# Attention B of a hybrid encoder block: its value products in two column halves, its row sums by a product with ones

## The chip, the cores and the metric

One core of a Trainium2 chip runs the whole program. The time is device microseconds from start to end of one execution; the medians are over three executions.

## The reference

One residual block on 1024 positions of width 1024, all in float32. A combined projection gives the inputs of two attention branches and two gates; the branches are projected, gated, added, projected again and added to x; then an MLP of width 4096. The change lies in branch B, eight heads of causal latent attention:

```python
s = jnp.einsum('bqhd,bkhd->bhqk', qi, k).astype(jnp.float32) * scale
s = jnp.where(key_chunk[None, :] <= q_chunk[:, None], s, -jnp.inf)
p = jax.nn.softmax(s, axis=-1).astype(v.dtype)
return jnp.einsum('bhqk,bkhd->bqhd', p, v)
```

Queries and keys have 96 numbers a head, values 64. Key chunks of 64 are causal as wholes.

## The kernel before, in words

All engines run lists of instructions written out by hand, which meet at semaphores. The stages follow one another: the input projection, the gates with attention A interleaved, attention B, the branch projections, the output projection, the MLP.

**Slots.** Attention B holds scores transposed, keys on partitions and queries along the free axis. A head has `HEAD_SLOTS` = 12 slots of one tile of 128 keys: slots 0 to 3 are the first half of the queries (512 of them) against key tiles 0 to 3, slots 4 to 7 the second half against key tiles 0 to 3 (full squares), slots 8 to 11 the second half against key tiles 4 to 7. The first and the last four are on the diagonal and have 512, 384, 256 and 128 columns. Eight heads make 96 slots. A slot number within a head is called r below.

**TensorE**, slot by slot (loop from L1698 on): `scores_t` makes the scores in three products of split numbers (L1638 to L1640) into one of two banks; `values_t` of the slot two before (L1643 to L1659) multiplies the exponentials with the values; `approx` (L1622) makes one chunk of the next head's approximate scores, whose row maxima DVE takes (`row_max`, L2090 to L2099) and SP moves into the row of queries; then come the steps of `preparations`: the projections of a later pair of heads (`group_step`, p 0 to 7) in the odd heads 1 and 3 and its transposes (p 8 to 15) in the even heads 2 and 4, for the second pair of heads both in head 0. Step p 7 falls into r 10 of an odd head (r 3 of head 0), p 12 into r 6 of the even head after it (r 9 of head 0).

**The value product** has 65 stationary columns, 64 of values and one of ones, so that row 64 of its result is the softmax's sum:

```python
out = PS[0:V_DIM + 1, 5 + u % 2, :]
ins = pe.matmul(out[:, c0:HALF], vB[g % 3][:, kt, h % B_GROUP, :], p_tile(t)[:, c0:HALF],
                start=kt == 0, stop=last)
```

**ScalarE** takes the exponentials (`exp_b`, L1321 to L1324), copies a half head's result out of its bank (`y_out`), and rounds it for the split (`y_high`, L1344). **SP** moves the sums from a row to a column (L718), stores the reciprocals (L723) and spreads them over 64 partitions (L728). **DVE** takes the reciprocals (L2105), multiplies (`y_norm`, L2115) and makes the low parts (`y_low`, L2122); each comes at a fixed slot of its own list. **GpSimd (POOL)** normalises the prepared queries and keys in a chain for each half of a group (`b_power`, `b_scale`, `b_rotate`, L879 to L984), which TensorE's transposes p 8 and p 12 wait for (`b_normed`); behind its second chain it splits attention A's output (L1012, L1014), and after the last chain it splits the branch weights (L870, L872).

**Behind the stage** come 16 branch products (`branch`, 24 products each, L1452). The fifth, e 4, waits for branch B's output (`yB_ready`), for its weights (`bw_ready`), and for the first gate multiplication (`gate_mul`), which DVE does after its last `y_low`. SP issues at the stage's end: three fetches of stored gates, the last sums, their reciprocals and the spread, a fourth gate, four loads of branch weights.

Of the kernel before, what the change touches and what calls it, by code (L numbers as in the profile page):

```python
# [62 lines left out]
P_RING = 3  # L63
# [24 lines left out]
def build(nc, x, positions, g_mix, w_in, b_gate, g_qa, g_ka, sinks_a, g_cq, g_ckv,  # L88
# [6 lines left out]
    with ExitStack() as ctx:  # L95
# [41 lines left out]
        b_sum = const("b_sum", [P, 2, Q_BLOCK])  # L137
# [6 lines left out]
        for t_ in (ident, b_gate_c, g_qa_c, g_ka_c, gqk_a, g_cq_c, g_ckv_c, g_qb_c, g_kb_c,  # L144
                   gqk_b, g_qr, g_kr, sink_r, pos_i, pos_c, inv_f, minus_half, x_ss, x_ms, x_rstd, z_ss, z_ms,
                   z_rstd, b_ss, b_ms, b_rstd, cos_t, sin_t, kr_rot, a_nmax, a_sum, a_rsum, b_nmax, b_part, b_sum,
                   b_rsum, probe):
# [50 lines left out]
        rtmp = [place(f"rtmp{i}", 199.875 + 0.5 * i, [P, 4, B_GROUP, RH]) for i in range(4)]  # L198
        vB = [place(f"vB{i}", (195.75, 202, 66.25)[i], [P, T, B_GROUP, V_DIM + 1]) for i in range(3)]
# [8 lines left out]
        p_diag = [place(f"p_diag{i}", 40 + 2 * i, [P, HALF]) for i in range(Q_BLOCK)]  # L208
        p_full = [place(f"p_full{i}", 48 + 2 * i, [P, HALF]) for i in range(P_RING)]
        r_row = [place(f"r_row{i}", 54 + 2 * i, [P, HALF]) for i in range(2)]  # L210
        y_raw = [place(f"y_raw{i}", 58 + 2 * i, [P, HALF]) for i in range(2)]

        yT_hi = [place(f"yT_hi{j}", (72, 76, 80, 84, 88, 128, 136, 140.75)[j], [P, S], F32R) for j in range(8)]
        yT_lo = [place(f"yT_lo{j}", (161, 165, 169, 173, 92, 132, 202, 144.75)[j], [P, S], F32R) for j in range(8)]
        b_raw = [place(f"b_raw{i}", 153 + 2 * i, [P, 4, P]) for i in range(BW_RING)]
# [32 lines left out]
        r_d = nc.dram_tensor("r_store", (2, P, Q_BLOCK), F32, kind="Internal").ap()  # L248
# [66 lines left out]
        v_one_ready = sem("v_one_ready")  # L315
# [7 lines left out]
        slot_done = sem("slot_done")  # L323
        y_raw_ready = sem("y_raw_ready")
        sum_landed = [sem(f"sum_landed{i}") for i in range(2)]
# [145 lines left out]
        def block_end(u):  # L471

            return HEAD_SLOTS * (u // 2) + (Q_BLOCK if u % 2 == 0 else HEAD_SLOTS)

        def diagonal(t):

            h, half, kt, c0 = slot(t)
            return kt >= Q_BLOCK * half

        def p_tile(t):  # L480

            h, half, kt, c0 = slot(t)
            return p_diag[kt - Q_BLOCK * half] if diagonal(t) else p_full[(Q_BLOCK * h + kt) % P_RING]

        def p_tile_before(t):

            h, half, kt, c0 = slot(t)
            if diagonal(t):
                return t - T if half else t - Q_BLOCK
            n = Q_BLOCK * h + kt - P_RING  # L490
            return HEAD_SLOTS * (n // Q_BLOCK) + Q_BLOCK + n % Q_BLOCK
# [15 lines left out]
        def chunk_at(t):  # L507

            h, r = t // HEAD_SLOTS, t % HEAD_SLOTS
            return N_CHUNKS * (h + 1) + r if h + 1 < B_HEADS else None  # L510

# [106 lines left out]
        def _(sp):  # L618
# [92 lines left out]
            def sum_row(u):  # L711

                r = 0 if (u // 2) % 2 else V_DIM
                return y_raw[u % 2][r:r + 1, :]

            def sum_move(u):
                sp.wait_ge(y_raw_ready, u + 1)
                sp.dma_start(b_sum[:, u % 2, :], sum_row(u).rearrange("o (p t) -> o p t", t=Q_BLOCK)  # L718
                             ).then_inc(sum_landed[u % 2], 16)

            def reciprocal_store(u):
                sp.wait_ge(rsum_b_ready, u + 1)
                sp.dma_start(r_d[u % 2], b_rsum[:, u % 2, :]).then_inc(r_stored, 16)  # L723

            def reciprocal_spread(u):
                s, r = u % 2, V_DIM * ((u // 2) % 2)
                sp.wait_ge(r_stored, 16 * (u + 1))
                sp.dma_start(r_row[s][r:r + V_DIM, :],  # L728
                             r_d[s].rearrange("p t -> (p t)").rearrange("(o q) -> o q", o=1).partition_broadcast(V_DIM)
                             ).then_inc(r_landed[s], 16)  # L730
# [19 lines left out]
            for h in range(B_HEADS):  # L750
# [4 lines left out]
                if h == 1:  # L755
                    for e in range(BW_RING):
                        branch_load(e)
                if more:
                    nmax_move(h + 1, 0, 1, 2)
                if h:  # L760
                    sum_move(2 * h - 1)
                if more:
                    nmax_move(h + 1, 3)
                if h:
                    reciprocal_store(2 * h - 1)
                if more:
                    nmax_move(h + 1, 4)
                if h:
                    reciprocal_spread(2 * h - 1)
                sum_move(2 * h)  # L770
                if more:
                    nmax_move(h + 1, 5)
                reciprocal_store(2 * h)
                if more:
                    nmax_move(h + 1, 6)
                reciprocal_spread(2 * h)
# [82 lines left out]
        def _(pool):  # L859
            pool.memset(ident[:, :], 0.0).then_inc(ident_ready, 1)  # L860
            pool.memset(minus_half[:, :], -0.5).then_inc(const_ready, 1)
            for i in range(RH):
                pool.memset(inv_f[:, i:i + 1], INV_FREQ[i]).then_inc(const_ready, 1)
# [152 lines left out]
            for n in range(2, 2 * B_GROUPS):  # L1016
# [3 lines left out]
                if n == 3:  # L1020
# [3 lines left out]
                    for j in range(4):  # L1024
                        yA_lanes(j)
# [10 lines left out]
            for e in range(2 * KD):  # L1036
                branch_splits(e)
# [1302 lines left out]
```

## Time and profile before

| | us |
|---|---|
| median of 3 runs | 1387.34 (1387.0 to 1388.23) |
| profiled execution, its own time | 1388.76 |
| its span, first to last instruction | 1386.9 |
| TensorE busy | 1364.9 (98%) |
| VectorE (DVE) busy | 814.6 (59%) |
| GpSimd (POOL) busy | 761.0 (55%) |
| ScalarE (ACT) busy | 407.8 (29%) |
| granted TensorE clock | 0.998 of full |

The profiled execution took 1.42 us more than the median. Busy times are unions over the whole span; attention B runs from 373 us to 545 us of it. A full float32 product leaves two records in the trace, a product of rounded float32 numbers one, so "x2" at a value product is one product. Starts of records are measured; the ends of matmul records are modelled and overlap the next record, so the chain's pieces are the better price of one product.

### The profile page before, as it was taken

How to read it: one execution, taken by the hardware profiler on the slowest of the kernel's cores; microseconds unless marked ns; L12 is line 12 of the kernel's file. 1: busy time of each engine (PE TensorE's matmuls, PEld its weight loads, DVE VectorE, ACT ScalarE, POOL GpSimd, SP SyncE). 2: the span in 40 equal slices, each digit the busy share in tenths (PEclk: the TensorE clock that was granted, in tenths of full speed). 3: DMA queues.
4: the chain of work that ended last, by engine and by line, in shares of the span. 5: the costliest groups of instructions: out<-in, count | busy, mean ns of one | idle time of the engine just before them, and what ended most of it. 6: DMA issues, size and time to landing. Idle time of an engine off the chain costs nothing.

```text
span 1386.9 us, 17629 instructions
## 1 busy us (share of the span) xinstructions
PE 1364.9 (98%) x6660; PEld 1119.9 (81%) x6660; DVE 814.6 (59%) x1422; ACT 407.8 (29%) x857; POOL 761.0 (55%) x618
## 2 busy tenths in 40 slices
PE   8999999999999999999999999999999999999998
PEld 8999887668867766888887888888888888888887
DVE  5401725743577773455356667777667776666776
ACT  5113235642355654000133212221221222221121
POOL 2341924445384520454308666668766667866697
PEclk9999999999999999999999999999999999999999
DMA  7120231211120012735101112111111221111113
GB/s 240 39 62 16 88 95 61 65 61 46 41 46 16 9 17 62 247 107 199 29 28 49 53 40 60 61 53 40 53 54 45 61 62 39 53 54 53 47 46 122
DMA packets 102884, 90.82 MB, mean 65 GB/s; under 512 B 21904, under 2 KB 84880, under 8 KB 102800
## 3 DMA queue, kind: packets, MB, share of 16 engines
q1 hardware_dynamic: 102656, 89.17, 21.0%
q8 instruction: 53, 0.87, 0.3%
q10 hardware_dynamic: 144, 0.52, 0.1%
q14 instruction: 31, 0.25, 0.1%
HBM read 76.99 MB, written 12.62 MB: 65 GB/s over the span
## 4 chain that ended last, share of the span: by engine, by line
PE 89%; POOL 3%; DVE 3%; ACT 2%; issue 1%; DMA 1%; ACTq 0%; DVEq 0%; POOLq 0%
PE PS L1452 76%; PE PS L1658 3%; PE PS L1459 2%; PE PS L1833 1%; PE PS L1553 1%; PE PS L1555 1%; PE PS L1638 1%; PE PS L1639 1%; PE PS L1622 1%; PE PS L1640 1%; POOL gw_lo L928 1%; DVE scA L2059 1%; POOL b_rstd L879 1%; PE PS L1575 1%; PE PS L1590 0%
## 5 line engine op out<-in xcount | busy, mean ns | idle before, releaser
L2243 DVE TENSOR_TENSOR xr<-PS,xr 128x512 f32<-128x512 f32 x240 | 161.9, 685 | 80.5 <-PE PS L1452 80.5
L2243 DVE TENSOR_TENSOR sum<-PS,sum 128x512 f32<-128x512 f32 x168 | 114.3, 687 | 91.3 <-PE PS L1452 91.3
L1452 PE MATMUL PS<-w_hi,u_hi 128*128 128x512 f32 x420 | 163.6, 390 | 0.8 <-DVE u_lo L2247 0.8
L1452 PE MATMUL PS<-w_lo,u_hi 128*128 128x512 f32 x420 | 163.4, 389 | 0.0
L1452 PE MATMUL PS<-w_hi,u_lo 128*128 128x512 f32 x420 | 163.4, 389 | 0.0
L1058 POOL TENSOR_TENSOR w_lo<-w_raw,w_hi 128x512 fp32r<-128x512 f32 x109 | 156.2, 1433 | 9.1
L1452 PE MATMUL PS<-mT_hi,w_hi 128*128 128x512 f32 x512 | 160.4, 389 | 0.0
L1452 PE MATMUL PS<-mT_hi,w_lo 128*128 128x512 f32 x512 | 160.2, 389 | 0.0
L1452 PE MATMUL PS<-mT_lo,w_hi 128*128 128x512 f32 x512 | 160.2, 389 | 0.0
L1387 ACT ACTIVATE relu_t<-PS 128x512 f32<-128x512 f32 x64 | 38.3, 599 | 296.7 <-PE PS L1452 293.8
L870 POOL TENSOR_SCALAR w_hi<-w_raw 128x1024 fp32r<-128x1024 f32 x32 | 39.4, 1230 | 155.7 <-DMA w_raw<-in_w_ff 155.7
L1452 PEld LDWEIGHTS PS<-mT_hi,w_lo 128*128 128x128 f32 x512 | 96.1, 188 | 20.0
L1452 PEld LDWEIGHTS PS<-mT_hi,w_hi 128*128 128x128 f32 x512 | 96.1, 188 | 19.9
L1452 PEld LDWEIGHTS PS<-mT_lo,w_hi 128*128 128x128 f32 x512 | 96.1, 188 | 19.9
L1452 PEld LDWEIGHTS PS<-w_hi,u_hi 128*128 128x128 f32 x420 | 78.8, 188 | 17.9 <-DVE u_lo L2247 1.6
L1395 ACT ACTIVATE u_hi<-u_raw 128x512 fp32r<-128x512 f32 x60 | 36.3, 629 | 191.4 <-DVE u_raw L2254 137.6
L1452 PEld LDWEIGHTS PS<-w_hi,u_lo 128*128 128x128 f32 x420 | 78.9, 188 | 16.4
L1452 PEld LDWEIGHTS PS<-w_lo,u_hi 128*128 128x128 f32 x420 | 78.9, 188 | 16.3
L1061 POOL TENSOR_TENSOR w_raw<-w_raw 128x512 f32<-128x512 f32 x60 | 80.1, 1336 | 18.2 <-PE PS L1452 15.2
L1452 PE MATMUL PS<-hT_hi,gw_hi 128*128 128x512 f32 x256 | 84.4, 411 | 3.5 <-ACT gate L1213 2.3
L1054 POOL TENSOR_SCALAR w_hi<-w_raw 128x512 fp32r<-128x512 f32 x109 | 87.7, 805 | 0.0
L2247 DVE TENSOR_TENSOR u_lo<-u_raw,u_hi 128x512 fp32r<-128x512 f32 x77 | 82.0, 1065 | 0.8 <-ACT u_hi L1390 0.8
(237 smaller groups left out, 2966.9 us busy)
## 6 DMA issues: line engine op xcount, KB each, us to landing
w_raw<-in_w_ff SPq DMA_DIRECT2D x32, 512.0 KB, 4.0
w_raw<-in_w_ff SPq DMA_DIRECT2D x64, 256.0 KB, 2.6
g_raw<-in_w_in SPq DMA_DIRECT2D x16, 512.0 KB, 3.9
gate_store<-gate SPq DMA_DIRECT2D x16, 512.0 KB, 2.6
x_in<-in_x SPq DMA_DIRECT2D x8, 512.0 KB, 10.7
gate_a<-gate_store SPq DMA_DIRECT2D x8, 512.0 KB, 7.6
gate_b<-gate_store SPq DMA_DIRECT2D x8, 512.0 KB, 4.8
raw<-in_w_out SPq DMA_DIRECT2D x8, 512.0 KB, 3.6
```

Of the source, the lines that this page charges most:

```text
L870: pool.tensor_scalar(hi_ap, raw_ap, 1.0, 1.0, ALU.mult, ALU.mult).then_inc(hi_done, 1)
L879: return pool.tensor_tensor(out_ap, in_ap, e, ALU.pow)
L1054: pool.tensor_scalar(w2_hi[b][:, :], w2_raw[b][:, :], 1.0, 1.0, ALU.mult, ALU.mult).then_inc(w2_step, 1)
L1058: pool.tensor_tensor(w2_lo[b][:, :], w2_raw[b][:, :], w2_hi[b][:, :], ALU.subtract).then_inc(w2_step, 1)
L1061: pool.tensor_tensor(w2_raw[AT[out]][:, :], w2_raw[AT[a]][:, :], w2_raw[AT[b]][:, :], ALU.subtract).then_inc(w2_step, 1)
L1387: act.activation(relu_t[:, :], PS[:, 2 * tile + half, :], ACT.Relu).then_inc(u_act, 1)
L1395: act.activation(u_hi[AT[p]][:, :], u_raw[AT[p]][:, :], ACT.Copy).then_inc(u_act, 1)
L1452: ins = pe.matmul(o, st, cut(mv), start=first and n == 0, stop=last and n == 2)
L1459: ins = pe.transpose(PS[0:rows, bank, i * P:(i + 1) * P], ap, ident[:, :])
L1658: ins = pe.matmul(out[:, c0:HALF], vB[g % 3][:, kt, h % B_GROUP, :], p_tile(t)[:, c0:HALF], start=kt == 0, stop=last)
L2243: dve.tensor_tensor(out, part, out, ALU.add).then_inc(acc_done, 1)
L2247: dve.tensor_tensor(u_lo[AT[p]][:, :], raw_ap, u_hi[AT[p]][:, :], ALU.subtract).then_inc(u_vec, 1)
```

## The change

The value tiles have 64 columns, without the ones. The twelve exponential tiles of a head have twelve places of their own (`p_set`, three sets of four) instead of four and a ring of three. The value products come in groups of four, one group every fourth slot at r 2, 6 and 10, for the four slots before; within a group they go by turns to PSUM partitions 0 to 63 and 64 to 127 of one bank. The two half results are added: ACT copies one out (`y_out`), DVE adds the other from PSUM (`y_add`).

For the sums, POOL adds the four tiles of the first set (`sums_first`, one multiplication and three additions) and those of the last set (`sums_last`, three additions), DVE adds the full tiles in pairs (`full_add`, two additions of 128x512). Four products with a 128x32 tile of ones, each into 32 partitions of the second half's bank, make the four sums (`sums`), at r 7 of the next head; for the last head behind branch product e 0. ACT copies that bank out, SP moves four rows, DVE adds three of them and takes two reciprocals. Multiplication, rounding and low parts come at slots 34 to 37 counted from the head's start. On POOL the additions stand between the chains; attention A's splits move to heads 5 and 6, the first four branch weight splits to heads 6 and 7, the loads of these weights to head 5 on SP.

```diff
             def y_out(u):
-                act.wait_ge(slot_done, block_end(u))
-                if u >= 2:
-                    act.wait_ge(yB_ready, u - 1)
+                act.wait_ge(group_done, 3 * h + 1 + 2 * half)
...
+            def sums_out(h):
+                act.wait_ge(s_done, h + 1)
+                if h:
+                    act.wait_ge(sum_landed, 64 * h)
+                act.activation(s_raw[:, :], PS[:, sums_bank(h), :], ACT.Copy).then_inc(s_read, 1)
...
+            def values_group(j):
+                h, part = j // 3, j % 3
+                half = min(part, 1)
+                u, g = 2 * h + half, h // B_GROUP
+                pe.wait_ge(p_ready, Q_BLOCK * (j + 1))
+                if part < 2 and u >= 2:
+                    pe.wait_ge(y_added, u - 1)
+                if part == 1 and h:
+                    pe.wait_ge(s_read, h)
...
+                for i in range(Q_BLOCK):
+                    own = (i % 2, i in (1, 2))[part != 1]
+                    c0 = P * i if part != 1 else 0
+                    rows = head_rows(h) if own else other_rows(h)
+                    ins = pe.matmul(PS[rows, 5 + half, c0:HALF], vB[g % 3][:, i + Q_BLOCK * (part == 2), h % B_GROUP, :],
+                                    p_set[part][i][:, c0:HALF], start=part < 2 and i < 2, stop=part != 1 and i >= 2)
+                ins.then_inc(group_done, 1)
+
+            def sums(h):
+                bank = sums_bank(h)
+                pe.wait_ge(sum_step, SUM_STEPS * (h + 1))
+                pe.wait_ge(full_added, 2 * (h + 1))
+                if h < B_HEADS - 1:
+                    pe.wait_ge(y_added, 2 * h + 2)
...
+                for i, p in enumerate((first_sum(h), p_sum[1], p_sum[2], p_set[2][0])):
+                    ins = pe.matmul(PS[32 * i:32 * i + 32, bank, :], ones_w[:, :], p[:, :], start=True, stop=True)
+                ins.then_inc(s_done, 1)
...
             for t in range(N_SLOTS):
                 scores_t(t)
-                if t >= 2:
-                    values_t(t - 2)
+                if t > Q_BLOCK and t % Q_BLOCK == 2:
+                    values_group(t // Q_BLOCK - 1)
                 a = chunk_at(t)
                 if a is not None:
                     approx(a)
+                if t > HEAD_SLOTS and t % HEAD_SLOTS == SUM_AT:
+                    sums(t // HEAD_SLOTS - 1)
                 for g, p in preparations(t):
                     group_step(g, p)
-            values_t(N_SLOTS - 2)
-            values_t(N_SLOTS - 1)
+            values_group(3 * B_HEADS - 1)
...
             for e in range(2 * KD):
                 branch(e)
+                if e == 0:
+                    sums(B_HEADS - 1)
...
+            chain(2)
+            chain(3)
+            sums_first(0)
+            for h in range(1, B_HEADS):
+                sums_last(h - 1)
+                sums_first(h)
+                if h in (1, 3):
+                    chain(h + 3)
+                    chain(h + 4)
...
+            def y_steps(t):
+                for h in range(B_HEADS):
+                    r = t - HEAD_SLOTS * h
+                    if r == 9:
+                        y_add(2 * h)
+                    if r == 17:
+                        y_add(2 * h + 1)
+                    if r in (10, 11):
+                        full_add(h, r - 10)
+                    if r == 24:
+                        sum_reciprocal(h)
+                    if r in (34, 35):
+                        y_norm(2 * h + r - 34)
+                    if r in (36, 37):
+                        y_low(2 * h + r - 36)
...
             for d in range(3):
                 fetch_a(d)
-            sum_move(BLOCKS - 1)
-            reciprocal_store(BLOCKS - 1)
-            reciprocal_spread(BLOCKS - 1)
+            reciprocal_store(B_HEADS - 2)
+            reciprocal_spread(B_HEADS - 2)
+            sum_move(B_HEADS - 1)
+            reciprocal_store(B_HEADS - 1)
+            reciprocal_spread(B_HEADS - 1)
             fetch_a(3)
```

## Rows read from the trace of the kernel before

**Rows 1.** The page: busy time by engine, and the chain by engine.
```profile
PE 1364.9 (98%) x6660; PEld 1119.9 (81%) x6660; DVE 814.6 (59%) x1422; ACT 407.8 (29%) x857; POOL 761.0 (55%) x618
...
PE 89%; POOL 3%; DVE 3%; ACT 2%; issue 1%; DMA 1%; ACTq 0%; DVEq 0%; POOLq 0%
```

**Rows 2.** Six heads: stretch, length, then PE, PEld, DVE, ACT, POOL busy us.
```profile
373.00:399.70 26.70, 24.60 (x126) 17.94 (x125) 20.10 (x61) 15.37 (x39) 22.94 (x26) 1.00 0.13 33
399.70:425.00 25.30, 25.30 (x123) 19.38 (x121) 17.93 (x63) 14.31 (x40) 18.64 (x16) 1.00 0.29 67
425.00:446.40 21.40, 20.68 (x106) 14.07 (x105) 17.49 (x44) 13.40 (x34) 10.20 (x11) 1.00 0.09 14
...
492.90:510.90 18.00, 17.13 (x74) 10.99 (x73) 12.56 (x31) 9.51 (x28) 7.56 (x7) 1.00 0.09 15
510.90:528.40 17.50, 16.84 (x74) 10.96 (x73) 11.04 (x30) 8.87 (x24) 0.00 (x0) 1.00 0.11 17
528.40:544.80 16.40, 15.61 (x66) 9.46 (x65) 4.65 (x10) 9.08 (x27) 0.00 (x0) 1.00 0.12 17
```
**Rows 3.** The chain of waits, heads 1 and 2: start, us, what.
```profile
424.29 0.55 ACT sqB L1265
...
426.36 2.92 POOL b_rstd L879
...
436.94 0.61 PE PS L1459 x4
437.79 0.24 PE PS L1639
438.26 0.86 PE PS L1658 x2
```

**Rows 4.** The chain in attention A, at its 64-column value products.
```profile
242.66 0.58 PE PS L1606 x4
```

**Rows 5.** Groups of instructions by shape: busy us, mean ns, idle before.
```profile
L1324 ACT ACTIVATE p_full<-PS 128x512 f32<-128x512 f32 x32 | 18.9, 596 | 4.9 <-PE PS L1640 4.5
...
L2122 DVE TENSOR_TENSOR yT_lo<-y_raw,yT_hi 64x512 fp32r<-64x512 f32 x14 | 9.8, 699 | 1.6 <-ACT yT_hi L1344 1.5
...
L2115 DVE TENSOR_TENSOR y_raw<-y_raw,r_row 64x512 f32<-64x512 f32 x14 | 11.7, 838 | 9.5 <-DMA r_row<-r_store 9.4
...
L972 POOL TENSOR_TENSOR q_nat<-q_nat,g_qr 128x256 f32<-128x256 f32 x4 | 2.9, 728 | 0.0
...
L2247 DVE TENSOR_TENSOR u_lo<-u_raw,u_hi 128x512 fp32r<-128x512 f32 x77 | 82.0, 1065 | 0.8 <-ACT u_hi L1390 0.8
```

**Rows 6.** POOL in order of time: the chain for step p 12 of head 0.
```profile
385.61 2.91 POOL L879 TENSOR_TENSOR b_rstd<-b_ms,minus_half 128x16 f32<-128x16 f32 x1 [0.40 <-DVE b_ms L2047]
...
394.64 0.45 POOL L984 TENSOR_TENSOR q_nat<-rtmp 128x128 f32<-128x128 f32 x1
```

**Rows 7.** Busy us by engine, r 7 to 11 of head 2.
```profile
437.30:446.40 9.10, 9.10 (x46) 6.00 (x45) 6.85 (x18) 5.42 (x13) 0.00 (x0) 1.00 0.08 17
```

**Rows 8.** SP's queue in order of time behind the stage.
```profile
546.30 0.75 SPq L718 DMA_DIRECT2D b_sum<-y_raw  x1
554.01 0.32 SPq L723 DMA_DIRECT2D r_store<-b_rsum  x1
555.42 0.47 SPq L728 DMA_DIRECT2D r_row<-r_store  x1
...
556.56 0.43 SPq L737 DMA_DIRECT2D b_raw<-in_w_branch_b  x1
```

**Rows 9.** DVE, then POOL, in order of time behind the stage.
```profile
561.53 0.69 DVE L2122 TENSOR_TENSOR yT_lo<-y_raw,yT_hi 64x512 fp32r<-64x512 f32 x1 [0.69 <-ACT yT_hi L1344]
...
562.68 0.62 POOL L870 TENSOR_SCALAR bw_hi<-b_raw 128x512 fp32r<-128x512 f32 x1 [61.97 <-DMA b_raw<-in_w_branch_b]
563.39 1.30 POOL L872 TENSOR_TENSOR bw_lo<-b_raw,bw_hi 128x512 fp32r<-128x512 f32 x1
```

**Rows 10.** The chain behind the stage: the branch products.
```profile
544.80 55.35 PE PS L1452 x244
```

More of the change, by code:

```diff
@@ L322, in build @@
         p_ready = sem("p_ready")
-        slot_done = sem("slot_done")
-        y_raw_ready = sem("y_raw_ready")
-        sum_landed = [sem(f"sum_landed{i}") for i in range(2)]
+        group_done = sem("group_done")
+        sum_step = sem("sum_step")
+        full_added = sem("full_added")
+        s_done = sem("s_done")
+        s_read = sem("s_read")
+        y_copied = sem("y_copied")
+        y_added = sem("y_added")
+        sum_landed = sem("sum_landed")
         rsum_b_ready = sem("rsum_b_ready")
@@ L1014, in yA_lanes, with chain @@
                 pool.tensor_tensor(yT_lo[j][:, :], yTa[:, j, :], yT_hi[j][:, :], ALU.subtract).then_inc(yA_split, 1)
-            for n in range(2, 2 * B_GROUPS):
+            def chain(n):
                 b_power(n)
@@ L1035, in branch_splits @@
                 split(b_raw[s][:, :, :], bw_hi[s][:, :, :], bw_lo[s][:, :, :], bw_hi_done, e + 1, bw_ready)
-            for e in range(2 * KD):
+            chain(2)
[7 more added lines that the diff above has]
+                    chain(h + 4)
+                if h == 5:
+                    pool.wait_ge(gate_done, 2 * KD)
+                    pool.wait_ge(pv_done, N_A // 2)
+                    pool.wait_ge(y_ready, N_A)
+                    for j in range(3):
+                        yA_lanes(j)
+                if h == 6:
+                    yA_lanes(3)
+                    branch_splits(0)
+                    branch_splits(1)
+                if h == 7:
+                    branch_splits(2)
+                    branch_splits(3)
+            sums_last(B_HEADS - 1)
+            for e in range(4, 2 * KD):
                 branch_splits(e)
@@ new lines, in y_add, with y_steps @@
+            def y_add(u):
+                h, half = u // 2, u % 2
+                c = 0 if half else P
+                y = y_raw[h // 2][head_rows(h), y_cols(half, c)]
+                dve.wait_ge(y_copied, u + 1)
+                dve.tensor_tensor(y, PS[head_rows(h), 5 + half, c:HALF], y, ALU.add).then_inc(y_added, 1)
+            def y_steps(t):
+                for h in range(B_HEADS):
+                    r = t - HEAD_SLOTS * h
+                    if r == 9:
[10 more added lines that the diff above has]
+                        y_low(2 * h + r - 36)
@@ L2147, in _ @@
             dve.wait_ge(gate_done, 2 * KD)
-            for i in range(Q_BLOCK):
-                dve.memset(p_diag[i][CHUNK:P, i * P:i * P + CHUNK], 0.0).then_inc(p_zero_ready, 1)
+            for part in (0, 2):
+                for i in range(Q_BLOCK):
+                    dve.memset(p_set[part][i][CHUNK:P, i * P:i * P + CHUNK], 0.0).then_inc(p_zero_ready, 1)
             for t in range(N_SLOTS):
```

273 lines of the change are left out of this document (141 added, 132 removed).

## The prediction

> **What bounds the kernel now.** The page first: TensorE is busy in 98% of the span and is 89% of the chain [rows 1], so only TensorE's own time, or a new wait of it, counts. The change touches 373 to 545 us, so next the busy time head by head [rows 2]. Head 1 has TensorE busy in all of its 25.30 us, DVE in 17.93. Head 2 has TensorE idle for 0.7 of 21.40 and DVE busy for 17.49; heads 5 and 6 have DVE at 12.56 of 18.00 and 11.04 of 17.50. Head 7, without approximations and preparations, has DVE at 4.65 of 16.40. The chain [rows 3] shows a second bound. From the projection copies of step p 7 (ACT, 424.29) through POOL's chain (from 426.36) to TensorE's transposes of p 12 (436.94) runs a latency of 12.65 us, and TensorE waits at its end. Head 0 has the same at r 9: POOL's second chain starts 0.4 us behind its first and ends at 395.09, whatever TensorE does before [rows 6].
>
> **Values.** One full value product takes 0.86 us of the chain [rows 3], so 0.43, 0.64 and 0.21 us for 256, 384 and 128 columns by proportion. A head has 4,608 columns in all: 9 x 0.86 = 7.74 us. Two 64-column products of 256 columns, side by side in attention A, took 0.58 us together [rows 4], where one after the other would be 2 x 0.43 = 0.86. So the halves do run at once, for 0.43 + 0.15 us of switching. I take 0.15 at either end of a group, 0.3 us. A group of four full tiles puts 1,024 columns on a side: 1.72 + 0.3 = 2.0 us; a diagonal one 640: 1.07 + 0.3 = 1.37. A head: 4.75 us, 3.0 less than now.
>
> **Sums.** Four products of 512 columns in four quarters: no row has 32-column tiles. All at once is 0.86 + 0.3 = 1.15 us; one after the other 3.4 + 0.3 = 3.7. I take 1.15, since rows 4 are the nearest and show no loss between two. TensorE's net per head is 1.9 us less.
>
> **DVE.** New per head: two 128x512 additions from SBUF, two from PSUM of 512 and 384 columns, a reduction. A 64x512 low part takes 0.70 us; 128x512 low parts in the MLP, beside a busy POOL, 1.07 [rows 5]. So a full addition is 0.70 to 1.07, the PSUM ones 0.69 and 0.55, the reduction with its link some 0.25: 2.9 to 3.6 us, I take 2.9. Its cover is DVE's idle time, large in heads 1 and 7, small in 2 and 5.
>
> **POOL.** 256 columns take 0.73 us [rows 5], so additions of 384, 256 and 128 about 1.0, 0.73 and 0.46 us: 2.2 us for a last set, 2.6 for a first one with its multiplication. They fit into heads 1, 3, 5, 6, 7, where POOL has over 6 us free [rows 2]. In the even heads the last set stands behind the chain.
>
> **ACT and SP.** ACT has one sum copy more and one-row copies less, 9 to 15 us busy of 16 to 27 [rows 2]; nothing. SP's 15 issues per head against 14, beside 16 us or more, cost nothing while the maxima go before the sums, as they do in its list.
>
> **Head by head.**
> Head 0: the wait at r 9 ends at 395.1 as before. Before, eight value products were done in its shadow; now the group of r 6 alone is, and that of r 10 comes behind it: 2.0 us against the 1.5 that slots 10 and 11 have now. **+0.5.**
> Heads 1 and 3, to step p 7 in r 10: now 7.1 us of value products; then the groups of r 2, 6, 10 and a sum, 1.37 + 1.37 + 2.0 + 1.15 = 5.9. -1.1; lean slots are as long for DVE as for TensorE, so I take **-0.8 each**.
> From p 7 to p 12 the 12.65 us stand: 0; TensorE only waits longer.
> Heads 2 and 4, r 7 to 11: 9.1 us, DVE 6.85 [rows 7]. TensorE has 4.1 us of values now, then 2.0 + 1.15, -0.9. DVE gets 0.69 + 1.4 more and loses 0.36: 8.6 of 9.1, so little of it comes through. The last set starts when the chain ends and takes 2.2 us plus its links, while TensorE gets to the sums about 1.3 us after the transposes: a wait of 1.0. **+0.9 each.**
> Head 5: DVE goes to 15.5, TensorE's 18.0 to 16.1; both are near. **-0.7.** Head 6: DVE 14 of 15.6: **-1.1.**
> Head 7: TensorE alone has scores 36 x 0.24 = 8.6 at most (narrow ones less: 6.8), values 4.75, sums 1.15, but lean slots are held by the exponential: three score products of 0.24, an exponential of 0.60 [rows 3, 5] and two hand-overs make 1.7 us per two slots, some 1.2 us of waits. The last group waits for the last exponential, 0.5. 14.4 for 16.40: **-2.0.**
>
> **Behind the stage.** The last head's sums stand among the branch products: **+1.15.** And what follows them is later. A branch product e takes 24 x 55.35/244 = 5.45 us [rows 10], so e 4 comes 21.8 us behind the end of the values, 23.0 with the sums. Now the spread is issued at +10.8 (555.42), the weights of e 4 land at +18.1 and are split at +20.1 [rows 8, 9]. New: sums done at +6.6, copied at +7.4, four moves issued by +9.7 and landed 2 us later, reciprocals at +12.3, stored, spread issued at +13.7 and +14.2, weights landed some 7 us behind: +21.4, split at +23.4. On DVE two norms and two low parts stand behind the spread's landing: last low part near +21, first gate multiplication 1.2 later. Today's sums were late because they queued behind the gate fetches (7.5 us from 546.30 to the reciprocal); the new ones come when these are through. A wait of 0 to 3 us; I take **+0.8.**
>
> **Sum:** 0.5 - 1.6 + 0 + 1.8 - 0.7 - 1.1 - 2.0 + 1.15 + 0.8 = -1.15 us, against 1388.76 of the profiled execution; against the median 1387.34 it makes 1386.2.
>
> **A rule against the change.** L2115 takes 0.84 us on average in the stage, where the same shape in L2122 takes 0.70 [rows 5]: some of its operations were held up. The Trainium skill, "SBUF — State Buffer", section "Who interferes with whom", says that a DVE operation with two SBUF inputs and a GpSimd one that reads SBUF exclude each other, the later one waiting in full. The new full additions and POOL's additions are of these kinds; it is the mechanism beside the second rival.
>
> **The rivals.**
> *TensorE's gain comes through where I let DVE take it* (chance 0.36). For it: rows 2 show DVE with slack in every whole head. Then -1.1 twice, -0.9 and no wait at the sums twice, -1.9 twice, -2.0, +0.5, +1.15, nothing behind: -8.1, 1379. Against it: DVE reads in order, and TensorE may be only two approximations ahead.
> *DVE becomes the bound* (0.23), the slower one. Place: r 7 to 11 of even heads and all of heads 5 and 6, where DVE and POOL now both work on SBUF. Price: full additions at 1.07, the eight y operations 0.15 longer each: 4.3 us per head. It decides when DVE's 8.6 of 9.1 us exceeds the stretch; 4.3 in place of 2.9 does. Then nothing is won in heads 1, 3, 5, 6, even heads lose 2.0 each, head 7 keeps -2.0, the tail waits 3: 0.5 + 4.0 - 2.0 + 1.15 + 3 = +6.7, 1394.
> *The quarters do not run at once* (0.04): 2.6 us more eight times, +20 less what hides: 1400 or more. Rows 4 speak against it.
> That the halves are not at once I leave out: rows 4 exclude it.
>
> **Numbers.** My case, within a few us of none, 0.37. About 0.2%, 2.8 us, is what a measurement of this kernel can tell from no change. Faster 0.36, same 0.37, slower 0.27. The range 1378 to 1394 holds both first rivals and leaves out the serial quarters and a full 15 us (8 x 1.9).
>
> **What would show it.** Value groups of 1.4 and 2.0 us and sums of 1.15 us in TensorE's order of time; longer waits for POOL's chain at r 9 of head 0 and r 6 of heads 2 and 4; TensorE waiting for POOL's additions at r 7 of these; DVE above 85% in heads 2 to 6; head 7 near 14.4 us; e 4 starting 23 us or more behind the last values. A DVE with idle time in heads 5 and 6 and a stage shorter by over 5 us would be the first rival; idle TensorE before approximations and transposes, with full additions of 1 us, the second.

## The result and the profile after

The changed kernel took 1400.99 us (median of 4 runs, 1399.63 to 1401.86) against 1387.76 us for the kernel before on the same chip: a ratio of 1.0092, with 95% interval 1.008 to 1.0104. It is slower, and the time lies outside the range. The profiled execution took 1401.86 us.

The page of after, busy time, granted clock and chain, which answers to [rows 1]:

```profile
PE 1363.9 (97%) x6724; PEld 1115.1 (80%) x6724; DVE 835.0 (60%) x1463; ACT 408.9 (29%) x857; POOL 799.3 (57%) x675
...
PEclk9999999999999998999999999999999999999999
...
PE 88%; DVE 5%; POOL 3%; ACT 2%; issue 1%; DMA 0%; DVEq 0%; POOLq 0%; ACTq 0%
```

Two things differ. DVE's share of the chain is 5% instead of 3%. And one slice of the clock row has an 8: TensorE did not have its full clock there. One slice is 35 us long, so this row hides short stretches. The windows by head of after (the columns are those of [rows 2], the last three being granted clock, DMA share and GB/s) show them:

```profile
371.84:402.39 30.55, 24.39 (x122) 17.30 (x121) 20.73 (x65) 15.68 (x39) 20.89 (x26) 0.89 0.11 29
402.39:426.15 23.76, 23.76 (x131) 18.24 (x129) 17.86 (x60) 13.36 (x38) 13.86 (x18) 1.00 0.09 16
426.15:447.63 21.48, 18.89 (x113) 12.95 (x112) 16.76 (x44) 12.49 (x32) 14.20 (x18) 1.00 0.09 14
447.63:472.93 25.30, 24.36 (x129) 18.11 (x128) 20.32 (x66) 14.11 (x42) 14.22 (x18) 1.00 0.09 12
472.93:496.72 23.79, 20.63 (x114) 13.93 (x112) 20.25 (x48) 13.97 (x34) 15.32 (x18) 0.93 0.09 13
496.72:514.99 18.27, 15.79 (x82) 9.84 (x80) 13.54 (x36) 8.98 (x27) 12.62 (x12) 1.00 0.31 74
514.99:539.51 24.52, 21.33 (x82) 13.62 (x81) 16.71 (x36) 9.01 (x26) 15.19 (x15) 0.72 0.08 11
539.51:556.22 16.71, 15.03 (x77) 8.48 (x75) 9.77 (x20) 10.07 (x29) 8.72 (x11) 1.00 0.13 24
```

The windows of the two heads of the kernel before that [rows 2] left out, 3 and 4:

```profile
446.40:471.60 25.20, 25.20 (x122) 19.26 (x121) 18.18 (x62) 14.37 (x42) 9.26 (x11) 1.00 0.08 12
471.60:492.90 21.30, 20.60 (x105) 14.04 (x104) 17.38 (x44) 13.28 (x34) 10.91 (x13) 1.00 0.09 14
```

From first score product to first branch product the stage takes 184.4 us; before it took 171.5 (373.0 to 544.5). Heads 0, 4 and 6 have a granted clock of 0.89, 0.93 and 0.72, and head 6 alone is 7.0 us longer. Windows over the stretches themselves:

```profile
392.90:399.80 6.90, 5.75 (x16) 2.55 (x17) 1.21 (x2) 1.07 (x3) 3.33 (x7) 0.51 0.01 0
478.30:481.70 3.40, 3.40 (x14) 2.16 (x12) 3.23 (x11) 2.01 (x6) 3.32 (x4) 0.50 0.03 3
519.20:532.90 13.70, 13.21 (x39) 8.95 (x40) 9.25 (x23) 4.21 (x11) 9.02 (x11) 0.50 0.12 20
```

They are at 0.5, the lower level of 1.2 GHz: 24.0 us in all, in which TensorE is busy for 22.4. At 2.4 GHz that work would have taken half as long, so by estimate they cost **about 11.2 us**. The kernel before has no such stretch in the stage (1.00 in each window). Without them the stage would take some 173.2 us, still 1.7 more than before. Two checks that half is the right price here: head 6 took 24.5 us with 13.7 us at half clock, and 18.4 with none in the run of the filled waits below; head 0 took 30.5 with 6.9 at half clock, and 27.8 with none.

The PE column gives the whole account. Its rows add up to 165.7 us busy of 171.5 before (up to the first branch product) and to 164.2 of 184.4 after. Take the clock's 11.2 us off, and TensorE's own work fell by 12.7 us; its idle time rose by 14.4, from 5.8 to 20.2. So the idle time alone is more than the gain, and the clock's 11.2 us come on top: 12.9 us in all.

What comes ahead of each stretch is idle time of TensorE. Its waits in after, in order of time:

```profile
394.05 1.06 PE L1525 MATMUL PS<-ident,q_nat 128*96 128x128 f32 x4 [2.65 <-POOL q_nat L995]
...
519.69 0.58 PE L1688 MATMUL PS<-kT_hi,qT_hi 96*128 96x256 f32 x1 [3.19 <-DVE b_part L2182]
```

The first is the wait at r 9 of head 0. The second stands at r 1 of head 6, and head 4 has its like at r 1 (2.4 us). Heads 2 and 5 wait there too, for 1.6 and 1.5 us, and no half clock follows. A sum of TensorE's waits over the stage shows what is new:

```profile
PE PS L1688 <- DVE b_part L2182: 9.2, 5, 3.2
PE PS L1525 <- POOL q_nat L995: 3.6, 3, 2.7
PE PS L1688 <- DVE b_nmax L2179: 3.3, 5, 1.1
```

The approximation (L1688) waits 12.5 us for DVE's row maxima; before it waited 1.1 us for them in the whole stage. What DVE does at that time is seen in its order of time before the wait in head 6:

```profile
514.62 0.69 DVE L2182 TENSOR_REDUCE b_part<-PS 128x1 f32<-128x512 f32 x1 [1.23 <-PE PS L1688]
515.34 0.69 DVE L2232 TENSOR_TENSOR y_raw<-y_raw,r_row 64x512 f32<-64x512 f32 x1
516.06 2.73 DVE L2192 TENSOR_TENSOR p_sum<-p_set,p_set 128x512 f32<-128x512 f32 x1
518.80 0.11 DVE L2176 MEMSET PS<- 64x64 f32 x1
518.94 0.69 DVE L2182 TENSOR_REDUCE b_part<-PS 128x1 f32<-128x512 f32 x1
519.67 0.15 DVE L2185 TENSOR_REDUCE b_nmax<-b_part 128x1 f32<-128x2 f32 x1
```

Behind the row maximum of r 10 stand the division (L2232) and a full addition (L2192). Only then comes the maximum of r 11 that the approximation of r 1 needs. This full addition takes 2.73 us, the other in this stretch 0.69. POOL is in its low part then:

```profile
515.42 2.82 POOL L1025 TENSOR_TENSOR yT_lo<-yTa,yT_hi 128x1024 fp32r<-128x1024 f32 x1
```

DVE's operation began 0.6 us behind it and ended 0.6 us behind its end. By the rule of the Trainium skill, "SBUF — State Buffer", section "Who interferes with whom", that the prediction cited, the later of two such operations is held until the first ends; this trace agrees (2.73 against 0.69 us).

**TensorE's own instructions cost what was forecast.** A diagonal group, the four ones products and a full group, in order of time:

```profile
430.73 1.30 PE L1727 MATMUL PS<-p_set,vB 128*64 128x512 f32 x8
...
440.44 0.63 PE L1743 MATMUL PS<-p_sum,ones_w 128*32 128x512 f32 x3 [0.78 <-POOL p_set L1035]
440.46 0.62 PE L1743 MATMUL PS<-p_set,ones_w 128*32 128x512 f32 x1
440.89 0.60 PE L1743 MATMUL PS<-p_sum,ones_w 128*32 128x512 f32 x3
...
469.07 1.94 PE L1727 MATMUL PS<-p_set,vB 128*64 128x512 f32 x8
```

1.30 and 1.94 us against 1.37 and 2.0; the two passes of the ones products start 0.45 us apart, some 1.0 us in all against 1.15. Head 1, where TensorE is busy throughout in both kernels, shows the net: 1.5 us less, against the 1.9 of the prediction.

### The profile page after: what moved, and what is told of

The parts are those of the page before. It is cut to its first block, busy times and chain, and to the rows that moved or that the text cites. A ratio compares the mean times of both kernels' runs of the same rounds, so it can differ in the third digit from the quotient of the medians.

```text
span 1400.0 us, 17848 instructions
## 1 busy us (share of the span) xinstructions
PE 1363.9 (97%) x6724; PEld 1115.1 (80%) x6724; DVE 835.0 (60%) x1463; ACT 408.9 (29%) x857; POOL 799.3 (57%) x675
## 4 chain that ended last, share of the span: by engine, by line
PE 88%; DVE 5%; POOL 3%; ACT 2%; issue 1%; DMA 0%; DVEq 0%; POOLq 0%; ACTq 0%
PE PS L1518 75%; PE PS L1727 2%; PE PS L1525 2%; PE PS L1921 1%; PE PS L1619 1%; PE PS L1688 1%; PE PS L1704 1%; PE PS L1705 1%; PE PS L1621 1%; PE PS L1706 1%; POOL gw_lo L939 1%; DVE scA L2145 1%; PE PS L1641 1%; PE PS L1743 1%; DVE p_sum L2192 1%
## 5 line engine op out<-in xcount | busy, mean ns | idle before, releaser
L1518 PEld LDWEIGHTS PS<-w_hi,u_hi 128*128 128x128 f32 x420 | 78.8, 188 | 18.1 <-DVE u_lo L2355 1.8
```

Source lines behind the costliest of these rows:

```text
L1518: ins = pe.matmul(o, st, cut(mv), start=first and n == 0, stop=last and n == 2)
```

## The experiments

The letters in the later texts on record: A and B are two theories of the waits at r 1, C and D two of the clock. Ratios are against the kernel before, with 95% interval. "Stage" is the length as above (before 171.5, after 184.4), "half" the time at half clock in it (0 and 24.0), both of the one profiled execution; where the stretches fall differs between executions, so medians carry the verdicts. The runs were made on several chips, on which the kernel before took 1386.4 to 1387.9 us: medians of different groups of runs compare to about 1.5 us only, and the ratios are the fairer measure.

| run | median us | ratio | stage, half |
|---|---|---|---|
| filled waits | 1400.31 | 1.0092 (1.0075 to 1.0109) | 182.6, 17.1 |
| additions at r 14, 15 | 1407.62 | 1.0134 (1.0117 to 1.0151) | 195.5, 37.5 |
| low parts in pieces | 1397.29 | 1.0076 (1.006 to 1.0093) | 179.0, 17.1 |
| late additions, pieces, fills in head 0 | 1409.52 | 1.0153 (1.0136 to 1.017) | 192.0, 27.3 |
| no full additions | 1399.51 | 1.0103 (1.0074 to 1.0132) | 178.0, 13.7 |
| full additions on POOL | 1400.96 | 1.0113 (1.0091 to 1.0134) | 181.6, 23.9 |
| splits two slots later | 1395.69 | 1.0065 (1.0046 to 1.0085) | 179.4, 27.3 |
| four edits at once | 1392.34 | 1.0045 (1.0028 to 1.0062) | 174.4, 10.2 |
| groups last in slot | 1397.97 | 1.0067 (1.005 to 1.0083) | 180.9, 27.3 |
| division four slots later | 1392.55 | 1.0038 (1.0024 to 1.0052) | 173.3, 10.2 |
| all edits together | 1391.57 | 1.0032 (1.0022 to 1.0043) | 173.1, 6.8 |
| before, DVE held, 16 | 1392.31 | 1.0039 (1.0026 to 1.0051) | 175.0, 3.4 |
| before, DVE held, 24 | 1396.07 | 1.0065 (1.0048 to 1.0082) | 180.2, 10.2 |
| division later, filled | 1393.75 | 1.0044 (1.0027 to 1.0061) | 177.5, 13.7 |
| division later, ones at r 8 | 1396.24 | 1.0064 (1.0048 to 1.0081) | 178.9, 3.4 |
| the same, ones at r 7 | 1391.01 | 1.0036 (1.0022 to 1.0051) | 173.3, 10.2 |
| division later, lanes moved | 1392.86 | 1.0046 (1.002 to 1.0071) | 178.3, 13.7 |
| additions where room is | 1389.17 | 1.0018 (1.0009 to 1.0027) | 170.8, 6.8 |

**Filled waits.** TensorE multiplies the identity with itself into a free bank ahead of three waits.

```diff
+                    if (g, p) == (1, 12):
+                        keep_busy(bank, 12)     # and 11, 14 of them at slots 49 and 73
```

> The changed kernel with 12, 11 and 14 small products of the identity on TensorE in front of the three long waits (head 0 r 9, head 4 r 1, head 6 r 1), about as long as the waits. Clock theory (the half clock behind the three idle stretches, 24 us long, costs about 10 of the 13 us): the granted clock stays at full from 373 to 560 us and the time falls to about 1391 us. Order theory (the waits themselves cost it): the waits are still there, filled, so 1401 us within 2.

No gain: the time is the one of the order theory. That does not show this theory, since the half clock did not go. Head 0 was free of half clock (27.8 us, 2.7 fewer), but stretches of 3.4 to 6.8 us stood in heads 2, 4 and 5. Filling single waits moved the stretches.

**Full additions at r 14 and 15.**

```diff
-                    if r in (10, 11):
+                    if r in (14, 15):
```

> The two full additions of a head move from r 10 and 11, where DVE also has the two y_norm, to r 2 and 3 of the next head. Order theory: TensorE's wait for DVE at r 1 (1.6, 0.5, 2.4, 1.5, 3.2 us in heads 2 to 6) shrinks by about 1.4 us each, 5 to 7 us in all. Clock theory: these too, and the half clock of heads 4 and 6 goes with them: 8.5 us more of it, 1388 to 1390 us; the half clock of head 0 stays. If DVE is bound by its amount of work and not by the order, the waits move to r 3 and 4 and the time stays at 1400.

Worse by 6.6 us. The exponential that overwrites these tiles in the next head now waits for the additions, and TensorE for it: the sum of waits of this kernel begins with

```profile
PE PS L1704 <- ACT p_set L1379: 7.1, 6, 1.6
```

**POOL's low parts in four pieces of 256 columns.**

```diff
-                pool.tensor_tensor(yT_lo[j][:, :], yTa[:, j, :], yT_hi[j][:, :], ALU.subtract)
+                for c in range(0, S, 256):
+                    ins = pool.tensor_tensor(yT_lo[j][:, c:c + 256], ...)
```

> The four GpSimd subtractions of 128x1024 in heads 5 and 6 become sixteen of 128x256. If the 2.73 us of DVE's full addition in head 6 is the hold of the GpSimd operation of 2.8 us beside it, that addition falls to at most 1.4 us and TensorE's wait of 3.2 us to about 2. Clock theory: head 6's half clock goes too, 7 us; in all 1392 to 1394 us. Order theory: 1399 to 1400 us.

Its DVE row in place of the one of 2.73 us:

```profile
515.78 1.10 DVE L2194 TENSOR_TENSOR p_sum<-p_set,p_set 128x512 f32<-128x512 f32 x1
```

The division in front of it took 1.36 us in place of 0.69, so the two together fell from 3.4 to 2.5 us, and TensorE's wait behind them from 3.2 to 2.3. A piece takes about 1.0 us, and the trace shows no operation held for longer than that. The median fell by 3.7 us, between the two forecasts; the intervals of the two ratios overlap, so the size is not certain. The late additions, the pieces and the fills of head 0 at once:

> The additions later, the short subtractions, and the 12 small products in head 0 alone, together. Clock theory: full clock throughout, stage shorter than before by a few us: 1383 to 1388 us. Order theory: 1392 to 1395 us. DVE bound by amount: 1396 us or more.

The late additions decide that one.

**No full additions.** They are cut to 8 columns, so the sums of the full tiles are left out of the output.

> The changed kernel with DVE's full additions cut to 8 of 512 columns (so the sums of the full tiles are left out of the softmax's division; everything else runs). It takes some 11 us of DVE work out of 8 heads, at the slots where TensorE waits for DVE. DVE theory (the full additions at r 10 and 11 make row_max late, TensorE waits at r 1, and behind the idle stretches the clock halves): the waits at r 1 of heads 2 to 6 fall from 1.7, 0.6, 2.6, 1.7, 3.3 us to under 1 each, the half clock of heads 4 and 6 goes, 1386 to 1391 us. Rival (the order of TensorE's groups itself leaves it short of work in these heads, DVE or not): the waits and the half clock stay for the most part, 1397 us or more.

Little: the ratio is no better than the change's, and the waits at r 1 of heads 2, 4 and 6 are still 1.05, 1.89 and 2.65 us (1.6, 2.4 and 3.2 before the cut). The additions are not the root. Beside them stood these two:

> The full additions go from DVE to POOL, behind sums_first, in heads 1 and 3 between the two chains, where POOL had 4.5 us free; two additions of 128x512, 2.7 us a head. DVE theory: like the run without them, 1387 to 1392 us. If POOL becomes the bound (its additions late at r 7 of heads 2 and 4), 1395 us and waits for POOL at the sums. A complete computation.

> ACT's y_high and DVE's y_low two slots later each (r 1 to 3 of the next head but two in place of r 11 to 1), the full additions stay. ACT's exponentials at r 0 and 1 then do not stand behind a y_high that waits for DVE's y_norm. If that coupling makes the wait at r 1, it falls by 1 us and more in heads 3 to 6 and the time to about 1394 us; if DVE's amount of work before row_max makes it, little changes, 1398 to 1401 us.

On POOL, the additions gain nothing. With the splits (`y_high`, `y_low`) moved by two slots the median is 5.3 us lower, of which 1.4 are the faster chip; the waits at r 1 of heads 3 to 5 stayed, and only that of head 6 fell, from 3.2 to 1.1 us. These two with the pieces and 12 fills in head 0:

> Full additions on POOL, y_high and y_low two slots later, the GpSimd subtractions of 1024 columns in quarters, and 12 small products before the wait of head 0. DVE theory with the clock's price: no half clock or one short one, 1382 to 1387 us, at or under the kernel before. If TensorE's order is the rest, 1390 us or more.

It took 1392.34 us, the second of its forecasts. POOL's additions are now late: TensorE waits 2.1 us for them at the ones products that stand in head 6.

**Groups last in their slot**, behind approximation and projection.

> The change, with TensorE's group of value products issued at the end of its slot, behind the maximum's product and the projection or transposes, instead of ahead of them. Theory A (with the full additions cut to nothing the waits of slot 1 stood at 1.2 to 2.8 us, so the additions are not their root: the group at r 10, 1.8 us, stands ahead of the product and of the projection that VectorE's row maximum of r 11 is queued behind): the waits of r 1 in heads 2 to 6, 1.6, 0.5, 2.4, 1.5 and 3.2 us, fall by up to 1.8 us each, no half-clock stretch is left but that of head 0, and the time is 1388 to 1392 us. Theory B (VectorE's division of y and the additions at r 10 and 11 hold the row maximum): the waits stay within 0.5 us of what they are, and the time is 1398 to 1402 us.

Theory A said 1388 to 1392, and it is 1398. Its waits at r 1 of heads 2 and 6 did go, to 0.15 and 0.16 us, but others came in their place:

```profile
434.14 0.61 PE L1525 MATMUL PS<-ident,q_nat 128*96 128x128 f32 x4 [1.36 <-POOL q_nat L995]
...
517.62 0.69 PE L1688 MATMUL PS<-kT_hi,qT_hi 96*128 96x384 f32 x1 [1.33 <-DVE b_nmax L2179]
```

The wait of head 4 fell to 1.0 us and that of head 5 to 0.9. So the group's place sets where TensorE waits, and little of how much.

**Division and splits four slots later** (ACT's `y_high` likewise, from 35 and 36 to 39 and 40).

```diff
-                    if r in (34, 35):
+                    if r in (38, 39):
                         y_norm(...)
-                    if r in (36, 37):
+                    if r in (40, 41):
                         y_low(...)
```

> The change, with the division of y and both splits of it four slots later, so that VectorE has only an addition beside the row maxima of r 10 and 11. Theory B: the waits of r 1 fall by 1.4 us each and the time is 1389 to 1394 us. Theory A: they fall by less than 0.7 us each, and the time is 1395 to 1401 us.

The most of any single edit: 8.4 us, the time that theory B had, and head 6 takes 18.1 us without any half clock. DVE's order at r 10 and 11 was most of the loss. The waits did not fall by 1.4 us each, as B said: at r 1 of heads 2, 4, 5 and 6 they went from 1.6, 2.4, 1.5 and 3.2 us to 1.57, 1.57, 0.94 and 0.44. What is left in head 2 is the group ahead of the projection, which A had right: with the group last it was 0.15.

> Everything together: groups last in their slots, full additions on GpSimd, splits two slots later, GpSimd's low parts in pieces of 256 columns and moved from heads 5 and 6 to heads 2 and 4, the ones products at r 8 instead of r 7, and 12 products of the identity into a free bank ahead of the wait of head 0. If idle time and the clock behind it are the whole loss, nothing is left but the gain that the costs of TensorE alone give: 1381 to 1386 us, with no half-clock stretch in the stage. If the change costs TensorE something that no wait shows, it stays at 1388 us or more.

It missed: 1391.57, no better than the single edit within the intervals. With the additions on POOL between sets and chains, the chain of head 2 was late.

**The clock in the kernel before.** DVE is held ahead of its row maximum of the first slot of heads 4 and 6.

```diff
+                if t in (48, 72):
+                    for k in range(16):
+                        dve.tensor_reduce(junk[:, k:k + 1], ident[:, :], AX.X, ALU.max)
```

> The kernel before, with VectorE held at two places only: 16 maxima over the identity, some 0.28 us each and 4.5 us together, ahead of its row maximum of the first slot of heads 4 and 6. TensorE's product of the slot after next waits for that maximum. Theory C (an idle stretch of about 3 us is followed by a stretch at half clock, whose price is half its length while TensorE streams): beside an idle time of 3 to 4 us at each place the trace shows half-clock stretches of 3.4 to 13.7 us behind them, and the time is 1387.5 plus 6 to 8 for the idle time plus 3 to 13 for the clock, so 1397 to 1408 us. Rival D (the clock's stretches come from something else in the changed kernel, its paired products or its burst of ones products): no half-clock stretch in the stage, and 1392 to 1395 us.

> The kernel before, VectorE held by 24 maxima over the identity instead of 16 at the same two places. With 16 of them TensorE stood idle for 2.3 and 2.1 us there, one stretch of 3.4 us at half clock followed, and it took 1392.31 us. Eight more at 0.19 us each are 1.5 us per place: 3.0 us more if idle time adds up alone, so 1395 us. Theory C (the longer the idle stretch, the more half clock behind it): half-clock stretches at both places, of 3.4 to 13.7 us each, and 1397 to 1403 us.

TensorE's wait and the window of the half clock behind it, with 16 in head 4:

```profile
476.68 0.45 PE L1623 MATMUL PS<-kT_hi,qT_hi 96*128 96x384 f32 x1 [2.15 <-DVE b_nmax L2094]
```

and with 24, the wait, and the windows of its two stretches and of the 89 us before them:

```profile
478.34 0.69 PE L1623 MATMUL PS<-kT_hi,qT_hi 96*128 96x384 f32 x1 [3.69 <-DVE b_nmax L2094]
```

```profile
478.10:484.90 6.80, 6.56 (x19) 4.63 (x20) 5.42 (x12) 3.10 (x7) 3.38 (x7) 0.50 0.06 1
522.40:525.90 3.50, 3.50 (x10) 2.52 (x9) 2.66 (x5) 2.41 (x6) 0.00 (x0) 0.51 0.06 1
381.00:470.00 89.00, 86.19 (x422) 62.62 (x420) 66.00 (x199) 50.87 (x134) 54.51 (x59) 1.00 0.13 26
```

This settles C against D: half clock comes in a kernel that has none of the changed products, behind an idle stretch that was put in. With 16, two waits of 2.15 and 1.96 us brought one stretch of 3.4 us, behind the first: the trace is C's, but the time, 1392.31, is one that D had named, since the reductions started 0.19 us apart, not 0.28, and the waits were shorter than meant. With 24, two waits of 3.69 and 3.50 us brought 10.2 us of half clock and 9.1 us more time, 1396.07, between idle time alone (1395) and C (1397 and more). Of the 8.7 us by which its stage is longer, 5.0 are the clock's (half of 10.1 busy).

**Versions with the division later.**

> The change with the division and the splits four slots later, as in the run of that edit (1392.55 us, half clock 3.4 us in head 0 and 6.8 us in head 4), and 12 products of the identity ahead of the wait of head 0. Theory C: the stretch of head 0 goes and 1 to 2 us with it: 1389.5 to 1392 us. Rival D: unchanged, 1392 to 1393 us.

> The change with the division and the splits four slots later, the full additions on GpSimd, GpSimd's low parts in 256-column pieces and moved to heads 2 and 4, the ones products at r 8, and the 12 products in head 0. Against the version of everything together (1391.57 us) the groups are back ahead in their slots and VectorE has nothing but row maxima and the projection's reads in r 10 to 1. Theory B (VectorE's order in r 10 to 1 makes the waits): 1383 to 1388 us, below the kernel before, with no half-clock stretch. If the waits of r 1 remain without any work of the change on VectorE, the values' new place on TensorE makes them, and it stays at 1388.5 to 1392 us.

> The version that took 1396.24 us with the ones products back at r 7. In that one they stood at r 8, their reading by ScalarE came after, and the values of r 10 waited for it, 7.2 us in six waits. Theory B: those 7.2 us go, 1 to 2 us for GpSimd's late additions at r 7 come back: 1387 to 1391 us. If it stays above 1392.5 us, the full additions on GpSimd are no gain behind the later division.

> The change with the division and the splits four slots later, and GpSimd's low parts in 256-column pieces and moved from heads 5 and 6 to heads 2 and 4; the full additions stay on VectorE. Theory B: the waits of heads 5 and 6 shorten against the version with the division alone later (1392.55 us, 17.5 and 18.1 us for these heads), and the time is 1389 to 1392.5 us; if GpSimd's work in heads 2 and 4 makes the ones products there wait, 1392.5 to 1395 us.

The 12 fills miss both forecasts and cost: head 0 takes 29.3 us with them, 27.9 without. Its stretch at half clock stands at 384.2, ahead of the fills, so it stayed; and with it TensorE comes so late to r 9 that the wait there is 1.1 us without fills, where 12 fills took 2.8 us in the run of the filled waits. The medians differ by 1.2 us, less than their intervals. Ones products at r 8 made a wait of their own, for ACT's reading of the bank:

```profile
PE PS L1747 <- ACT s_raw L1408: 7.2, 6, 1.4
```

That version has 3.4 us at half clock only, and its stage is still 7.4 us longer than that of the kernel before: waits alone cost most of that. Back at r 7 the time falls by 5.2 us. The low parts in pieces and moved to heads 2 and 4, without the other edits, show nothing (1392.86 against 1392.55).

**Each addition where there is room**: full additions on POOL in heads 2, 4, 5, 6 and 7, which have no chain, else on DVE; division four slots later; low parts in pieces and moved.

> The division and the splits four slots later, GpSimd's low parts in 256-column pieces and moved to heads 2 and 4, and the full additions on GpSimd in the heads where it has no chain (2, 4, 5, 6, 7), on VectorE in heads 0, 1 and 3. Against the version with all of them on GpSimd (1391.01 us; heads 5, 6 and 7 at 16.9, 17.0 and 15.9 us, below the 17.9, 17.5 and 16.2 of the kernel before, head 4 at 25.6 with 6.8 us of half clock behind a late chain) the chain of head 4 is early again: 1386 to 1389 us, within 0.2% of the kernel before, if the clock is granted but for head 0; 1389 to 1391 us if a stretch of head 4 stays. Below 1384 us would say that all of the predicted gain of TensorE's instructions can be had; above 1391 us that the place of the additions does not matter.

It is the best version: 1389.17 us, 11.8 us under the change. With a ratio of 1.0018 (1.0009 to 1.0027) it is still a little slower than the kernel before. Its windows for heads 3 to 7:

```profile
445.02:468.71 23.69, 23.69 (x129) 18.16 (x128) 19.32 (x64) 13.99 (x42) 20.37 (x26) 1.00 0.09 13
468.71:492.52 23.81, 20.64 (x113) 14.07 (x112) 20.89 (x48) 13.50 (x34) 21.12 (x24) 0.93 0.07 13
492.52:508.79 16.27, 15.84 (x81) 9.88 (x80) 12.39 (x34) 9.03 (x27) 13.77 (x16) 1.00 0.36 83
508.79:526.80 18.01, 16.28 (x81) 10.03 (x80) 13.45 (x34) 8.87 (x26) 10.00 (x12) 1.00 0.11 16
526.80:542.65 15.85, 14.92 (x78) 8.44 (x76) 5.75 (x15) 8.90 (x27) 13.23 (x15) 1.00 0.17 24
```

Heads 3, 5 and 7 are 1.5, 1.7 and 0.3 us under those of the kernel before. Head 6 is 0.5 above and head 4 2.5. Its stage of 170.8 us has 6.8 us of half clock. Those of head 4 cost 1.7 by half the busy time. Those of head 0, at 384.9, cost next to nothing: the wait for POOL at r 9 behind them is 1.1 us in place of 2.65, and the head takes 27.87 us, where the filled one without half clock took 27.8. So some 169 us would be left without them, 2.4 under before. TensorE's own work is 11.7 us less than before and its idle time 7.6 us more, 13.5 for 5.8. The gain in TensorE's instructions is there, but the waits took most of it and the clock the rest, and no version here beat the kernel before.

## Why the prediction was wrong

Its sum was made against 1388.76 us and gave 1387.6 for a profiled execution; it was 1401.86, a miss of 14.3. Per head, with half of TensorE's busy time at half clock taken off:

| head | forecast | measured | so corrected |
|---|---|---|---|
| 0 | +0.5 | +3.9 | +1.0 |
| 1 | -0.8 | -1.5 | -1.5 |
| 2 | +0.9 | +0.1 | +0.1 |
| 3 | -0.8 | +0.1 | +0.1 |
| 4 | +0.9 | +2.5 | +0.8 |
| 5 | -0.7 | +0.3 | +0.3 |
| 6 | -1.1 | +7.0 | +0.4 |
| 7 | -2.0 | +0.5 | +0.5 |
| behind | +1.95 | +1.4 | +1.4 |

(Head 7 is measured here to the first branch product's record in both kernels, 16.2 and 16.7 us.)

- **The step that failed first: DVE's cost was set against its idle time ("Its cover is DVE's idle time"), and from that came "lean slots are as long for DVE as for TensorE" and no wait at all at r 1.** The amount was even too high: DVE is busy for 16.6 us more in the stage, 2.1 per head for the 2.9 of the prediction. What counted was the order. In r 10 to 1 DVE has the division, the addition and the low parts in one bundle, where the kernel before had them spread, while TensorE has three slots without values. So TensorE waits 12.5 us for row maxima in place of 1.1. That costs heads 3, 5 and 6 what they should have gained: +0.1, +0.3 and +0.4 with the clock's part taken off, against -0.8, -0.7 and -1.1. Moving the division and the splits alone gave 8.4 us back.
- **The term that was left out: the clock.** Idle time of TensorE was priced at its length and no more ("TensorE only waits longer"), and the clock was among neither the costs nor the rivals. It cost 11.2 us more: 2.9 behind head 0's wait for POOL's chain, which the prediction had, and 8.3 behind the two waits of 2.4 and 3.2 us for row maxima, which it had not. The place of which it says "the 12.65 us stand: 0" did no harm: at p 12 TensorE waits 0.2 us in head 2, and none is shown in head 4. [Rows 2] had shown the clock at 1.00, and no wait of the kernel before in the stage was over 1.12 us; that such an engine has something to lose was there to be read.
- **Port**: the second rival had the mechanism (full additions held), but priced it at 1.07 us each. Their mean was 0.81, and one of 2.73 came at the worst place. The rival's own price, DVE as the bound, was wrong too: DVE is busy in 68 to 85% of heads 2 to 6. It bound by its order, not by its load. The rival's sign, idle TensorE before the approximations, did come. Its 4.3 us per head fit four y operations that are held, the two multiplications and the two low parts; with the eight that it names they would be 4.8.
- **Head 7**, +0.5 for -2.0. It holds four groups, since head 6's last one falls into it (1.3 us that I left out), and two waits for exponentials of 0.8 and 0.4 us beside the small ones.
- **Right**: the groups, the ones products, the wait for POOL's additions at r 7 of head 2 (0.8 us for 1.0; head 4 shows none), the 1.15 us among the branch products (1.1). The tail's 0.8 us did not come: e 4 starts at 579.3, 23.1 us behind the values, no wait of TensorE is shown there, and its weights are split 1 us ahead:

```profile
576.27 0.62 POOL L881 TENSOR_SCALAR bw_hi<-b_raw 128x512 fp32r<-128x512 f32 x1 [16.99 <-DMA b_raw<-in_w_branch_b]
576.97 1.30 POOL L883 TENSOR_TENSOR bw_lo<-b_raw,bw_hi 128x512 fp32r<-128x512 f32 x1
```

Together: clock 11.2, waits and the rest of the stage 4.8, tail -0.5 and an earlier start of the stage, 371.8 for 373.0, that the held kernels of before have too: -1.2. That is the 14.3 us.

Two things stay open. Why one idle stretch is followed by 3.4 us of half clock, a longer one by 13.7 and others by none was not found out; the length of the stretch does not decide it alone, as the last section shows. And what share of the 8.4 us is the clock and what share the waits by themselves can only be read off single profiles.

## What to carry to other kernels

When TensorE runs at full clock with idle stretches of 1.1 us at most, a change that saves its work by gathering it into bursts is not free where it then waits: look where the new gaps of some 1.6 us or more will be, or several shorter ones close together, and price them above their own length. Ask of each helper engine not only whether it has time, but what stands in its queue in front of the one result that TensorE needs next. And after moving work away from a hot spot, check which buffer is now freed late: additions four slots later cost 6.6 us, ones products one slot later 5.2.

## What the hardware showed that was not expected

- Two idle stretches of TensorE were put into a kernel with a clock of 1.00 in the stage. Of 2.15 and 1.96 us, the first was followed by 3.4 us at half clock and the second by none; of 3.69 and 3.50 us, by 6.8 and 3.5.
- The same wait is sometimes followed by half clock and sometimes not. A wait of 1.57 or 1.58 us at r 1 of head 2 or 4 stands twelve times in the profiled executions, and behind five of them, within 2 us of the wait's end, the clock fell.
- Half clock ahead of a wait for another engine can be free: in the best version 3.4 us of it in head 0 only shortened the wait for POOL behind it.
- Four 32-column products of 512 float32 columns, each into a quarter of one bank, start within 0.02 us of each other; a pass of all four takes 0.45 us, where a pass of one value product took 0.43 [rows 3].
- A few short waits in a row can come ahead of it as well. In the best version, 3.4 us at half clock begin at 384.9, behind these; the kernel before has waits of 0.3 and 0.7 us there, with values between them, and keeps its clock. But the same three waits stand in 16 of the profiled executions of changed kernels, and the clock fell behind them in 12; the change itself (waits of 0.84, 1.12 and 0.69 us) is one of the four that kept it. TensorE's waits in order of time, then the window:

```profile
379.08 0.89 PE L1631 MATMUL PS<-wuq,cqT 128*128 128x192 f32 x4 [0.84 <-DVE vB L2117]
383.14 0.33 PE L1700 MATMUL PS<-kT_hi,qT_hi 96*128 96x128 f32 x1 [1.11 <-DVE b_nmax L2191]
384.16 0.61 PE L1537 MATMUL PS<-ident,q_nat 128*96 128x128 f32 x4 [0.69 <-POOL q_nat L995]
```

```profile
384.90:388.30 3.40, 3.40 (x12) 1.61 (x10) 1.31 (x5) 1.20 (x2) 3.32 (x2) 0.50 0.04 5
```
